# Banks, order of the own tile and one ScalarE copy in the attention stage of a streaming encoder layer

## The reference

```python
h = rms_norm(x, ln1); proj = h @ w_in
q, k, v, f, xr, yg = split(proj)             # 8 heads of 64; 512 recurrent channels
q = rms_norm(q, q_gain); k = rms_norm(k, k_gain)
logf = log_sigmoid(f + b_f)
# attention: logit[t,s] = q_t.k_s/8 + c_t - c_s, c = cumsum(logf), s <= t; softmax; @ v
# prompt: over its 1024 frames; streams: over 512 cached frames and their own 16
xc = causal_conv(xr); hs = rg_lru(xc)
mixed = concat(rms_norm(attn), rms_norm(gelu(yg) * hs))
x = x + mixed @ w_out
x = x + square(relu(rms_norm(x, ln2) @ w_up)) @ w_down
```

## Time and profile before

| | |
|---|---|
| Median of 3 runs | 1526.71 us (1524.6 to 1527.34) |
| Profiled execution, its own time | 1524.6 us |
| Its span, first to last instruction | 1522.6 us |
| TensorE busy | 1426.3 us, 94% of the span |
| VectorE busy | 731.5 us, 48% |
| ScalarE busy | 419.6 us, 28% |
| Mean granted TensorE clock | 0.971 of full speed |
| HBM read and written | 78.28 MB and 9.71 MB |

### The profile page before, as it was taken

One profiled execution on the slowest core, in us unless ns is written; L12 is line 12 of the kernel. 1 busy time (PEld: TensorE's weight loads), 2 busy tenths in 40 slices (PEclk: granted clock), 3 DMA queues, 4 the chain that ended last, 5 costly groups with the idle time before them and its releaser, 6 DMA issues.

```text
span 1522.6 us, 19612 instructions
## 1 busy us (share of the span) xinstructions
PE 1426.3 (94%) x7683; PEld 1213.6 (80%) x7691; DVE 731.5 (48%) x1186; ACT 419.6 (28%) x749; POOL 83.1 (5%) x120
## 2 busy tenths in 40 slices
PE   4979999999998993998999999999999999999997
PEld 3764856849577882887989998999889998999886
DVE  6364353544534547664444444444444444444444
ACT  5124233242325556232312211122112211221110
POOL 2510101101000000000000000000000000000000
PEclk7889999999999996999999999999999999999998
DMA  6022423333242113011101110111111110111004
GB/s 187 8 66 74 121 79 99 102 86 92 63 119 53 30 58 126 29 42 56 56 29 56 55 41 17 51 55 41 41 28 55 41 41 28 55 55 41 27 15 125
DMA packets 129547, 92.95 MB, mean 61 GB/s; under 512 B 14679, under 2 KB 119127, under 8 KB 129493
## 3 DMA queue, kind: packets, MB, share of 16 engines
q1 hardware_dynamic: 129492, 92.20, 21.2%
HBM read 78.28 MB, written 9.71 MB: 58 GB/s over the span
## 4 chain that ended last, share of the span: by engine, by line
PE 88%; DVE 4%; DMA 4%; ACT 2%; issue 1%; SPq 1%; POOL 0%; DVEq 0%
PE psum L1496 25%; PE psum L1497 25%; PE psum L1498 25%; DMA k_c<-in_cache_k_dram 3%; PE psum L1730 2%; PE psum L1681 2%; PE psum L1712 1%; PE psum L1715 1%; PE psum L1740 1%; PE psum L1831 1%; PE psum L1562 1%; DVE tops L1219 1%; PE psum L1609 1%; PE psum L1852 0%; POOL rs L709 0%
## 5 line engine op out<-in xcount | busy, mean ns | idle before, releaser
L1464 DVE TENSOR_TENSOR mix<-psum,mix 128x512 f32<-128x512 f32 x288 | 196.4, 690 | 163.4 <-PE psum L1498 163.3
L1496 PE MATMUL psum<-h_hi,wu_hi 128*128 128x384 f32 x768 | 259.3, 338 | 4.2 <-DVE mix L1418 4.2
L1498 PE MATMUL psum<-h_hi,wu_lo 128*128 128x384 f32 x768 | 259.0, 337 | 0.0
L1497 PE MATMUL psum<-h_lo,wu_hi 128*128 128x384 f32 x768 | 259.0, 337 | 0.0
L1496 PE MATMUL psum<-wd_hi,u_hi 128*128 128x512 f32 x576 | 225.4, 391 | 3.6 <-issue 3.6
L1497 PE MATMUL psum<-wd_lo,u_hi 128*128 128x512 f32 x576 | 225.3, 391 | 0.0
L1498 PE MATMUL psum<-wd_hi,u_lo 128*128 128x512 f32 x576 | 225.1, 391 | 0.0
L1496 PEld LDWEIGHTS psum<-h_hi,wu_hi 128*128 128x128 f32 x768 | 145.2, 189 | 4.9 <-issue 4.4
L1497 PEld LDWEIGHTS psum<-h_lo,wu_hi 128*128 128x128 f32 x768 | 145.1, 189 | 0.5
L1498 PEld LDWEIGHTS psum<-h_hi,wu_lo 128*128 128x128 f32 x768 | 145.1, 189 | 0.0
L993 ACT CAST wd_hi<-raw 128x1024 fp32r<-128x1024 f32 x32 | 32.1, 1049 | 401.2 <-PE psum L1498 399.9
(11 more groups left out here) (262 smaller groups left out, 2066.0 us busy)
## 6 DMA issues: line engine op xcount, KB each, us to landing
raw<-in_w_up_dram SPq DMA_DIRECT2D x32, 512.0 KB, 4.5
raw<-in_w_down_dram SPq DMA_DIRECT2D x32, 512.0 KB, 3.4
k_c<-in_cache_k_dram SPq DMA_DIRECT2D x32, 256.0 KB, 3.2
raw<-in_w_in_dram SPq DMA_DIRECT2D x32, 192.0 KB, 4.0
out_dram<-mix SPq DMA_DIRECT2D x9, 512.0 KB
x_in<-in_x_prompt_dram SPq DMA_DIRECT2D x8, 512.0 KB, 4.1
v_c<-in_cache_v_dram SPq DMA_DIRECT2D x16, 256.0 KB, 4.3
kts<-in_cache_v_dram SPq DMA_DIRECT2D x16, 256.0 KB, 3.9
```

Of the source, the lines that this page charges most:

```text
L1464: nc.vector.tensor_tensor(at, psum[:, 4 + 2 * (t % 2) + half, :].rearrange("p (k n) -> p k n", n=P), at, ALU.add).then_inc(y_added, 1)
L1496: nc.tensor.matmul(out, hi(k), r_hi(k), start=first and k == 0, stop=False)
L1497: nc.tensor.matmul(out, hi(k), r_lo(k), start=False, stop=False)
L1498: last = nc.tensor.matmul(out, lo(k), r_hi(k), start=False, stop=end and k == n - 1)
```

## The change

- Values and sums of the second half go to banks 0 and 1; the streams' scores (`S_SCORES`) to 6 and 7, with their turned weights, outputs and two banks of the recurrent chunk 0 changed to suit.
- TensorE turns the own tile at u = 3, ahead of `turn_tops`, not at u = 5. values(4) waits for all 13 high and 9 low parts.
- ScalarE copies `q_own` between exp(7) and exp(8), not behind exp(13), and copies stream 2's keys behind exp(21), not behind exp(23).
- VectorE makes queries and keys of a head's low part together (`low`). Both heads' low parts of the second half lie ahead of maximum (0, 7); the keys had come after the shifts. `k_own` comes ahead of the first denominators.

```diff
-    S_SCORES = 0
+    S_SCORES = 6
     def weights_bank(g):
-        return 6 if g == 0 else 0
+        return 0 if g == 0 else 6
     def sample_out_bank(g):
-        return 7 if g == 0 else 0
+        return 1 - g
     def lru_banks(c):
-        return ((4, 5, 3), (2, 6, 1), (0, 7)) if c == 0 else ((0, 1, 2), (3, 4, 5), (6, 7))
+        return ((4, 5, 3), (2, 6, 7), (0, 1)) if c == 0 else ((0, 1, 2), (3, 4, 5), (6, 7))
...
-                for s in range(STEPS):
+                for s in range(8):
+                    exp(s)
+                act.wait_ge(qk_turned, NT * p + NT)
+                nc.scalar.activation(q_own[:], psum[:, 0, 0:P], ACT.Copy, scale=qgain[:, 0:1]).then_inc(hi_done, 1)
+                for s in range(8, STEPS):
                     exp(s)
                     if s == 9:
                         outputs(0)
-                    if s == 13:
-                        act.wait_ge(qk_turned, NT * p + NT)
-                        nc.scalar.activation(q_own[:], psum[:, 0, 0:P], ACT.Copy, scale=qgain[:, 0:1]).then_inc(hi_done, 1)
...
-                    if s in (19, 23):
-                        sample_past(p, (s - 19) // 2)
+                    if s in (19, 21):
+                        sample_past(p, s - 19)
...
-                def low_queries(t, hp):
+                def low(t, hp):
                     r, other, g = head_rows(hp), head_rows(1 - hp), t // 4
+                    qb, kb, _ = turned_banks(t)
+                    n = slice(g * SPAN, (g + 1) * SPAN)
                     dve.wait_ge(hi_done, HI_PAIR * p + (2 * hp + 2 if g == 0 else 2 * hp + 10))
...
+                    nc.vector.scalar_tensor_tensor(cross_qk[other, g, 0, hp, :], psum[r, qb, :], qgain[r, 0:1],
+                                                   QA[r, hp, n].bitcast(F32), ALU.mult, ALU.subtract).then_inc(lo_done, 1)
+                    nc.vector.tensor_tensor(cross_qk[r, g, 1, hp, :], psum[r, kb, :], KA[r, hp, n].bitcast(F32),
+                                            ALU.subtract).then_inc(lo_done, 1)
...
                 bound(0, 6)
-                low_queries(4, 0)
+                low(4, 0)
                 bound(1, 6)
+                low(4, 1)
                 bound(0, 7)
-                low_queries(4, 1)
                 bound(1, 7)
                 shift(0, 1)
                 shift(1, 1)
-                low_keys(4, 0)
-                low_keys(4, 1)
-                denominators(0)
                 dve.wait_ge(qk_turned, NT * p + NT)
                 nc.vector.tensor_copy(k_own[:], psum[:, 1, 0:P]).then_inc(lo_done, 1)
+                denominators(0)
...
                 if g == 0:
                     pe.wait_ge(q_blocks_ready, 2 * p + 2)
-                    pe.wait_ge(lo_done, NT * p + NT)
+                    pe.wait_ge(bound_read, 20 * p + 20)
...
                     if s == 8:
-                        pe.wait_ge(lo_done, NT * p + 6)
+                        pe.wait_ge(lo_done, NT * p + 8)
...
-                    if s == 16:
-                        pe.wait_ge(lo_done, NT * p + 8)
...
+                    if s == 8:
+                        pe.wait_ge(hi_done, HI_PAIR * p + HI_PAIR)
+                        pe.wait_ge(lo_done, NT * p + NT)
                     pe.wait_ge(exp_done, STEPS * p + s + 2)
...
-                        last = nc.tensor.matmul(psum[r, 4 if qc == 0 else 6, a0 - qc * SPAN:SPAN], v1[:, kt, r],
+                        last = nc.tensor.matmul(psum[r, 4 if qc == 0 else 0, a0 - qc * SPAN:SPAN], v1[:, kt, r],
...
-                        last = nc.tensor.matmul(psum[32 * i:32 * i + 32, 5 if qc == 0 else 7, a0 - qc * SPAN:SPAN], ones_s[:],
+                        last = nc.tensor.matmul(psum[32 * i:32 * i + 32, 5 if qc == 0 else 1, a0 - qc * SPAN:SPAN], ones_s[:],
...
-                    if u == 5:
+                    if u == 3:
                         turn_qk(NT - 1)
-                    if u == 3:
                         turn_tops(0, 1)
                         turn_tops(1, 1)
                         scores(8)
```

More of the change, by code:

```diff
@@ L859, in outputs @@
                     act.wait_ge(pv_done, 12 * p + (4 if qc == 0 else 12))
-                    nc.scalar.copy(mix[:, p, qc * SPAN:(qc + 1) * SPAN], psum[:, 4 if qc == 0 else 6, :]).then_inc(o_copied, 1)
+                    nc.scalar.copy(mix[:, p, qc * SPAN:(qc + 1) * SPAN], psum[:, 4 if qc == 0 else 0, :]).then_inc(o_copied, 1)
                 if p == 0:
@@ L1237, in denominators @@
                     else:
-                        nc.vector.tensor_copy(dens[:, 1, :], psum[:, 7, :]).then_inc(den_copied, 1)
+                        nc.vector.tensor_copy(dens[:, 1, :], psum[:, 1, :]).then_inc(den_copied, 1)
                 for t in range(NT):
@@ L1246, in pair_dve @@
                             dve.wait_ge(stored, 16 * NT)
-                        for hp in range(2):
-                            low_queries(0, hp)
-                            low_keys(0, hp)
+                        low(0, 0)
+                        low(0, 1)
                     if t == 6:
```

## The result

The changed kernel takes 1534.11 us (median of 6 runs) against 1525.65 for the kernel before: a ratio of 1.0053, 95% interval 1.004 to 1.0066. By the ratio it is 8.1 us slower, between 6.1 and 10.1; the two medians lie 8.5 apart. The profiled execution took 1530.25, with a span of 1528.5. It flatters the change a little: TensorE's granted clock over the first 80 us, ahead of anything that was changed, was 0.98 of full in it and 0.83 in the profile of before, and pair 0 comes to turn_tops(1,0) 0.8 us sooner.

What follows compares the result with a forecast made beforehand. TensorE was taken as the bound, 88% of the chain that ended last. The terms +2.4 - 0.8 + 4.2 = +5.8 us, on a median of 1526.7, gave 1532.5 us, range 1530.5 to 1535.

Steps and rivals of the forecast that it cites:

- Part 1: VectorE at u = 3: low parts ahead of the last two maxima; +0.60 us per pair, +2.4 in all.
- The flush behind each operation: Rival on VectorE's low parts: operations hold the next one back; +11.6 us, 1538.3; chance 0.03.
- Part 2: TensorE: own tile's turn from u = 5 to u = 3, hidden there; -0.19 us per pair, -0.8 in all.
- values(4): TensorE's new wait for q_own and k_own: slack 1.1 us or more, cost 0.
- Part 3: ScalarE's copy of past stream 2 behind exp(21) makes values(11) 1.22 us later per pair; +4.2 us after absorbed transfer waits.
- Transfers gave nothing back: Rival at the tail: earlier transfers of streams 5 to 7 return up to 3.6 us; 1528.9; chance 0.10.
- Banks: Second half's swapped banks: same instructions, sizes and order; cost 0.
- The granted clock: TensorE's clock in the attention stretches: stays 1.00 despite another 1.8 us of idle; no cost.
- the 0.7 that was counted: Transfer waits at turn_past(3), 0 to 0.36 us per pair, taken as absorbing part of the copy's delay.
- ScalarE did not pace the second half: Rival: ScalarE's 1.67 us between exp(13) and exp(14) sets the pace, 6.7 come back; 1526.6, no change; chance 0.04.
- nothing was hit harder: Rival: late transfers of stream 5 and the values collide, one more us per pair; 1536.5; chance 0.08.

Runs made afterwards that it cites:

- the keys in the gap: Changed kernel with head 1's low keys made between maximum (0,7) and maximum (1,7), not ahead of (0,7); ratio 1.0013 against the kernel before.
- the third pair of banks: Changed kernel with stream 2's copy behind exp(23), bound (1,7) in free banks 0 and 1, own tile's turn behind the tops' transposes; ratio 0.9968.
- the kernel with the copy back and the keys in the gap: Changed kernel with stream 2's copy behind exp(23) and head 1's low keys between maxima (0,7) and (1,7); ratio 0.9994 against the kernel before.
- the padded kernel: Changed kernel with eight matmuls that nobody reads put ahead of bound (1,7) at u = 3; ratio 1.0028 against the kernel before.

## Why the prediction was right or wrong

The forecast, 1532.5, lies 1.6 below the measured 1534.11, and the sign and the range hold. In terms of the difference it was too small: 5.8 forecast, 8.1 measured (6.1 to 10.1). The time looks closer than the difference because the forecast started from a median of 1526.7 for the kernel before, which is 1525.65 with three more runs. Point by point:

- **Part 1, +0.60 per pair:** right, 0.65 at full clock (19.34 to 19.99). That the gap between (0,7) and (1,7) gives nothing back was right as well: VectorE idled 0.90 there in pair 0 and 1.43 in pair 1, at half clock. The flush behind each operation, which would have made it more, is against the rows: 215.89 to 216.68 is 0.79 from queries to keys, and the next starts 0.73 later.
- **Part 2, -0.19 per pair:** mis-sized, -0.31 (20.91 to 20.60). The turn at u = 3 was hidden, narrowly, as worked out. In pair 0 the weight sums of u = 5 and scores(14) start 1.00 apart instead of 1.19, so the turn gives its 0.19. Of the rest 0.10 lies at scores(13): before it started just behind the end of exp(11) (132.29, and 132.35), and with the change exp(11) ends 0.14 sooner behind the tops' transposes. No run tries this.
- **values(4):** no wait, right.
- **Part 3, +4.2:** the mechanism was right to the instruction, the size 3.4. The two short exponentials take 0.45 together in all four pairs and not the 0.58 of the earlier trace rows, so values(11) came 1.68 and not 1.80 behind turn_past(2), with 1.02 as the wait. From turn_past(2) to (3) that makes 1.03 more in pair 0, where 1.22 was forecast. Transfers gave nothing back: turn_past(3) to the next pair is 51.00, 51.07 and 50.42 against 50.89, 51.33 and 50.58. Four pairs of kernels price it. The copy moved by itself costs 4.9 (the change), 5.3 (the kernel before), 2.9 (with the keys in the gap) and 3.7 (with the third pair of banks), and only in the last was neither profile at half clock.
- **Banks:** nothing that can be measured, right, by the kernel with the copy back and the keys in the gap.
- **The sum of these** is 2.6 - 1.2 + 3.4 = 4.8, and the changed kernel with TensorE kept busy measures 4.3 (2.4 to 6.1).
- **The granted clock:** the step that failed. I wrote that it "is 1.00 in the attention stretches in spite of 4 us of TensorE idle in 44; another 1.8 should not change that", and gave it no price. The 1.00 over 44 us was read in a kernel without the longer wait, and it says nothing about the place that matters: the change puts 0.65 us more wait exactly where TensorE already idled most. From the stretches, pairs 1 and 2 lost 1.24 each at u = 3 beyond the 20.00 of the padded kernel, pair 3 0.72 there and 0.85 behind it: about 4.1 us. The padded kernel gives 3.8 by the ratios. The rest of the forecast was 1.0 too large (5.8 against 4.8), so the two errors partly hide each other: 4.8 and about 4 make 8.8, within the interval of the 8.1 measured. That 1534.11 lies inside the forecast's range is in part luck: about half of the measured cost came from a term that was put at nothing. Why the clock falls in some pairs and not in others stays open.

The rivals: the transfers gave back nothing worth naming beyond the 0.7 that was counted (the fourth row of the table is 0.3 shorter in all), ScalarE did not pace the second half (its wait for the turn vanished and the stretch moved by 0.3 per pair), and nothing was hit harder. The Trainium skill's sum of 2.0 us plus bytes over 436 GB/s (DMA: Bandwidth & Descriptors, Anatomy of one DMA) is its fit to transfers that GpSimd issues. Here SP issues them, and in the changed kernel those of past keys took 2.7 to 5.4 us from issue to landing, 3.0 in the median, where the sum gives 2.6.

## What to carry to other kernels

When a change lengthens a wait, look at what stands around it: on TensorE 0.65 us more in a place that idled already cost 1.9 us in pairs 1 and 2, because the clock fell behind it. Work put ahead of another engine's data is free only as far as it fits the idle gap there (1.48 us did not fit 0.90), and a copy that waits for the next stage must not stand in front of the last work of this one. Moving TensorE's work into an earlier wait gains nothing while another engine's chain sets the next start, and here the clock fell in more pairs for it; shorten that chain, as the free pair of banks did. Edits that are harmless alone can make a new wait together, as the turn behind the low keys did (0.95 us per pair), so replay the queues once more for the combination.

## What the runs showed of the hardware

The clock fell from 2.4 to 1.2 GHz inside a stage in which TensorE was idle for no longer than 1.97 us at a time (1.32 in the kernel before with the copy moved), with real matmuls between the waits, and in some pairs of one execution but not in others of the same code. Once down it stayed there for several us although TensorE was busy most of the time: in the kernel with VectorE's order alone, 9.20 of 10.50 us at 0.51. The Trainium skill (TensorE: Matmul & The Clock Gate, What's actually happening) says that the clock depends on how busy TensorE has been of late; the padded kernel agrees around u = 3, where 1.9 us of matmuls that nobody reads kept it at 1.00 in all four pairs and the time came out 3.8 us below that of the change.
